# One scan stage of an encoder layer: smaller score blocks on TensorE, a mask moved within VectorE's order, and a subtraction moved to GpSimd

## What is computed

```
# one direction, per head: q, k, log f are 128 channels, v is 128 channels
b       = cumsum(log_f within the chunk)
o_inter = (q * exp(b)) @ state
scores  = q_t . k_s * exp(b_t - b_s)   for s <= t within the chunk, else 0
o       = o_inter + scores @ v
state   = exp(b_last) * state + (k * exp(b_last - b))^T @ v

kv      = rms_norm(memory) @ w_ckv     # 512 rows x 1024 times 1024 x 2048
```

## Time and profile before

| | us |
|---|---|
| median of 3 runs | 2024.71 (2020.85 to 2026.29) |
| the profiled execution | 2023.5 |
| its span, first to last instruction | 2021.7 |
| first and last TensorE work of `hgrn` | 460.25 to about 686.9 |

### The profile page before, as it was taken

One profiled execution on the slowest core, in us unless ns is written; L12 is line 12 of the kernel. 1 busy time (PEld: TensorE's weight loads), 2 busy tenths in 40 slices (PEclk: granted clock), 3 DMA queues, 4 the chain that ended last, 5 costly groups with the idle time before them and its releaser, 6 DMA issues. The chain is left out here.

```text
span 2021.7 us, 32126 instructions
## 1 busy us (share of the span) xinstructions
PE 1940.0 (96%) x11104; PEld 1609.6 (80%) x11104; DVE 1467.0 (73%) x2035; ACT 1225.7 (61%) x1962; POOL 277.2 (14%) x391
## 2 busy tenths in 40 slices
PE   7989999999999899999999999999999999999995
PEld 6878888887888676778888888887888888888882
DVE  5447765648999588877411355468999999999985
ACT  5453467427788488754222333336888888888873
POOL 0220012110000021111000000001222222222210
PEclk9999999999999999999999999999999999999997
DMA  6493334446565460343334523337999999999998
GB/s 207 162 313 109 105 115 146 151 172 180 181 183 178 151 199 27 116 135 134 115 120 138 163 84 110 116 132 272 384 386 382 384 378 382 380 386 383 394 370 323
DMA packets 177237, 441.98 MB, mean 219 GB/s; under 512 B 20768, under 2 KB 100000, under 8 KB 151264
## 3 DMA queue, kind: packets, MB, share of 16 engines
q1 hardware_dynamic: 145168, 341.19, 47.1%
q0 software_dynamic: 31952, 99.25, 13.3%
HBM read 359.64 MB, written 94.37 MB: 225 GB/s over the span
## 5 line engine op out<-in xcount | busy, mean ns | idle before, releaser
L113 PE MATMUL cross_ot_ps<-w_w_high,cross_o_high 128*128 128x512 f32 x528 | 213.4, 404 | 4.6 <-DVE w_w_low L2952 2.8
L115 PE MATMUL cross_ot_ps<-w_w_high,cross_o_low 128*128 128x512 f32 x528 | 207.1, 392 | 0.0
L2952 DVE TENSOR_TENSOR cross_low_up<-cross_raw_up,w_w_high 128x2048 fp32r<-128x2048 f32 x66 | 148.3, 2288 | 9.4 <-ACT w_w_high L2719 9.3
L2952 DVE TENSOR_TENSOR w_w_low<-cross_raw_gate,w_w_high 128x2048 fp32r<-128x2048 f32 x68 | 152.3, 2278 | 0.0
L2952 DVE TENSOR_TENSOR cross_low_down<-cross_raw_down,w_w_low 128x2048 fp32r<-128x2048 f32 x64 | 143.4, 2282 | 0.0
L2719 ACT ACTIVATE w_w_high<-cross_raw_gate 128x2048 fp32r<-128x2048 f32 x68 | 126.2, 1907 | 0.0
L113 PEld LDWEIGHTS cross_ot_ps<-w_w_high,cross_o_high 128*128 128x128 f32 x528 | 99.9, 189 | 29.9 <-DVE w_w_low L2952 7.1
L2719 ACT ACTIVATE w_w_high<-cross_raw_up 128x2048 fp32r<-128x2048 f32 x66 | 122.5, 1907 | 0.3 <-issue 0.3
L2719 ACT ACTIVATE w_w_low<-cross_raw_down 128x2048 fp32r<-128x2048 f32 x64 | 119.0, 1914 | 0.0
L115 PEld LDWEIGHTS cross_ot_ps<-w_w_high,cross_o_low 128*128 128x128 f32 x528 | 99.7, 189 | 21.5
L114 PE MATMUL cross_ot_ps<-w_w_low,cross_o_high 128*128 128x512 f32 x264 | 104.2, 395 | 0.0
(11 more groups left out here) (539 smaller groups left out, 5495.1 us busy)
## 6 DMA issues: line engine op xcount, KB each, us to landing
cross_raw_gate<-in_w_gate_dram SPq DMA_DIRECT2D x66, 1024.0 KB, 7.7
cross_raw_up<-in_w_up_dram SPq DMA_DIRECT2D x66, 1024.0 KB, 9.5
cross_raw_down<-in_w_down_dram SPq DMA_DIRECT2D x64, 1024.0 KB, 9.0
front_pair_raw<-in_w_in_dram SPq DMA_DIRECT2D x9, 1024.0 KB, 7.0
cross_y_kept<-y_rows SPq DMA_DIRECT2D x16, 512.0 KB, 10.4
front_raw<-in_w_in_dram SPq DMA_DIRECT2D x10, 512.0 KB, 5.5
k_t<-front_staged POOLq DMA_DIRECT2D x20, 256.0 KB, 2.7
lf_t<-front_staged_lf POOLq DMA_DIRECT2D x20, 256.0 KB, 3.0
```

What stands on the lines that cost most here:

```text
L113: pe.matmul(out, lhs[0], rhs[0], start=first, stop=False)
L115: return pe.matmul(out, lhs[1], rhs[0], start=False, stop=last)
L2952: dve.tensor_tensor(w_low[s][:, cols], raw[s][:, cols], w_high[s][:, cols].bitcast(F32), ALU.subtract).then_inc(w_low_done[s], 1)
```

## The change

Six edits, all in `hgrn`:

1. Level scores are computed only where they are not zero: one 64x64 block per head at level 64, two 32x32 blocks per head at level 32. Level 16 stays at four 32x32 blocks per head, each with its zeros. Each block has `start=True` and `stop=True`, and there is no adding up over levels.
2. The centred scores are four 32x32 blocks per head in place of one 128x128.
3. The level scores have a PSUM buffer for each direction and the centred scores a bank of their own. Both are set to zero once by VectorE at the start of the stage (two memsets, 128x1024 and 128x512), for the parts that no block writes. TensorE waits for them before slot 0.
4. GpSimd sets 4 halves to zero in place of 12.
5. `decayed` is cut in two, `decayed_levels` (the six half multiplies) and `decayed_rest`, and `mask(n+1)` is put between them, where before `mask(n+1)` came first in the next slot.
6. `split_low` is done by GpSimd for all of the parts 2 to 15, ahead of the DMA of part p - 2.

```diff
-        kt_ps, o_ps, st_ps = (m.ps(s, [P, HW]) for s in ("kt_ps", "o_ps", "st_ps"))
-        s_ps = m.ps("s_ps", [P, 2, 2, HEADS // 2, P])
+        kt_ps, o_ps, st_ps, centred_ps = (m.ps(s, [P, HW]) for s in ("kt_ps", "o_ps", "st_ps", "centred_ps"))
+        levels_ps = m.ps("levels_ps", [P, 2, HW])
 ...
             def _(pool):
                 for t, half in ((q_dec, early), (k_dec, late)):
                     for u in range(2):
-                        for j, w in enumerate(LEVELS):
-                            halves = t[:, u, j].rearrange("p (g two l) -> p g two l", two=2, l=w)
-                            pool.memset(halves[:, :, half[u]], 0.0).then_inc(zeros_done, 1)
+                        halves = t[:, u, n_lev - 1].rearrange("p (g two l) -> p g two l", two=2, l=base)
+                        pool.memset(halves[:, :, half[u]], 0.0).then_inc(zeros_done, 1)
+
+                def split_low(p):
+                    pool.wait_ge(w_high_done, p - 1)
+                    pool.tensor_tensor(w_low[p % 2][:], raw[p % 2][:], w_high[p % 2][:].bitcast(F32),
+                                       ALU.subtract).then_inc(w_low_done, 1)
+
                 for p in range(parts):
+                    if p + 2 < parts:
+                        split_low(p + 2)
 ...
-                    act.activation(by_head(s_t[:]), levels_ps, ACT.Copy).then_inc(level_scores_done, 1)
+                    act.activation(s_t[:], levels_ps[:, u], ACT.Copy).then_inc(level_scores_done, 1)
 ...
             def _(dve):
                 dve.sem_inc(base_done, PRIME)
+                dve.memset(levels_ps[:].rearrange("p u c -> p (u c)"), 0.0).then_inc(levels_zeroed, 1)
+                dve.memset(centred_ps[:], 0.0).then_inc(levels_zeroed, 1)
 ...
-                decayed(0, 0)
+                decayed_levels(0, 0)
+                decayed_rest(0, 0)
                 dve.memset(state[:], 0.0).then_inc(state_done, PRIME)
-                split_low(2)
                 differences(1, 0)
                 mask(0, 0)
-                decayed(0, 1)
-                split_low(3)
+                decayed_levels(0, 1)
+                decayed_rest(0, 1)
                 for n in range(slots):
-                    if n:
-                        mask(n // 2, n % 2)
                     if n + 3 < slots:
                         differences((n + 3) // 2, (n + 3) % 2)
                     carry(n // 2, n % 2)
                     if n + 2 < slots:
-                        decayed(n // 2 + 1, n % 2)
-                    for p in range(4, parts):
-                        if split_in[p] == n:
-                            split_low(p)
+                        decayed_levels(n // 2 + 1, n % 2)
+                    if n + 1 < slots:
+                        mask((n + 1) // 2, (n + 1) % 2)
+                    if n + 2 < slots:
+                        decayed_rest(n // 2 + 1, n % 2)
 ...
-                        pe.wait_ge(zeros_done, 4 * n_lev)
+                        pe.wait_ge(zeros_done, 4)
+                        pe.wait_ge(levels_zeroed, 2)
 ...
+                    def block(into, j, h, s_at, t_at, size):
+                        rows, cols = (slice(h * P + at, h * P + at + size) for at in (s_at, t_at))
+                        return pe.matmul(into[s_at:s_at + size, cols], k_dec[:, u, j, rows], q_dec[:, u, j, cols],
+                                         start=True, stop=True)
+
+                    wide, narrow = LEVELS[0], 2 * base
                     for h in range(HEADS):
-                        cols = slice(h * P, (h + 1) * P)
-                        pe.matmul(s_ps[:, h % 2, 1, h // 2], k_dec[:, u, n_lev, cols], q_dec[:, u, n_lev, cols],
-                                  start=True, stop=True)
-                    for pair in range(HEADS // 2):
-                        for j, w in enumerate(LEVELS):
-                            for h in (2 * pair, 2 * pair + 1):
-                                for at in range(0, P, 2 * w):
-                                    cols = slice(h * P + at, h * P + at + 2 * w)
-                                    done = pe.matmul(s_ps[at:at + 2 * w, h % 2, 0, pair, at:at + 2 * w],
-                                                     k_dec[:, u, j, cols], q_dec[:, u, j, cols],
-                                                     start=(j == 0), stop=(j == n_lev - 1))
+                        block(levels_ps[:, u], 0, h, early[u] * wide, late[u] * wide, wide)
+                    for h in range(HEADS):
+                        for at in range(0, P, 2 * narrow):
+                            block(levels_ps[:, u], 1, h, at + early[u] * narrow, at + late[u] * narrow, narrow)
+                    for h in range(HEADS):
+                        for at in range(0, P, narrow):
+                            block(levels_ps[:, u], n_lev - 1, h, at, at, narrow)
+                    for h in range(HEADS):
+                        for at in range(0, P, narrow):
+                            done = block(centred_ps, centred, h, at, at, narrow)
                     done.then_inc(scores_ready, 1)
```

More of the change, by code:

```diff
@@ L1167, in hgrn @@
         raw, w_high, w_low = zip(*early_split)
-        kt_ps, o_ps, st_ps = (m.ps(s, [P, HW]) for s in ("kt_ps", "o_ps", "st_ps"))
-        s_ps = m.ps("s_ps", [P, 2, 2, HEADS // 2, P])
-        by_head = lambda t: t.rearrange("p (a b t) -> p a b t", b=2, t=P)
-        levels_ps, centred_ps = (s_ps[:, :, c].rearrange("p b a t -> p a b t") for c in range(2))
+        kt_ps, o_ps, st_ps, centred_ps = (m.ps(s, [P, HW]) for s in ("kt_ps", "o_ps", "st_ps", "centred_ps"))
+        levels_ps = m.ps("levels_ps", [P, 2, HW])
         acc = m.ps("acc", [P, 2, 512])
@@ L1177, in hgrn @@
         o_stored = [m.sem(f"o_stored{u}") for u in range(2)]
-        (scan_done, zeros_done, diff_done, decay_done, base_done, scores_ready, level_scores_done, s_done,
-         kt_done, o_ready, o_done, state_done) = (
+        (scan_done, zeros_done, levels_zeroed, diff_done, decay_done, base_done, scores_ready,
+         level_scores_done, s_done, kt_done, o_ready, o_done, state_done) = (
             m.sem(s) for s in (
-                "scan_done", "zeros_done", "diff_done", "decay_done", "base_done", "scores_ready",
-                "level_scores_done", "s_done", "kt_done", "o_ready", "o_done", "state_done"))
+                "scan_done", "zeros_done", "levels_zeroed", "diff_done", "decay_done", "base_done",
+                "scores_ready", "level_scores_done", "s_done", "kt_done", "o_ready", "o_done", "state_done"))
         def token(i, u):
@@ L1356, in differences, with decayed_levels @@
                                       ALU.subtract).then_inc(diff_done, 1)
-                def decayed(i, u):
+                def decayed_levels(i, u):
                     n = 2 * i + u
@@ L1361, in decayed @@
                     if n == 0:
-                        dve.wait_ge(zeros_done, 4 * n_lev)
+                        dve.wait_ge(zeros_done, 4)
                     dve.drain()
@@ L1371, in decayed, with decayed_rest @@
                         dve.tensor_tensor(kd[:, :, early[u]], e[:, :, early[u]], halves(k)[:, :, early[u]], ALU.mult)
+                def decayed_rest(i, u):
+                    n = 2 * i + u
+                    q, k = x[i % 2][:, u, 0], x[i % 2][:, u, 1]
                     dve.tensor_tensor(q_dec[:, u, n_lev], q, decay[:, u, centred], ALU.mult)
@@ L1384, in mask @@
                     dve.wait_ge(level_scores_done, n + 1)
-                    dve.copy_predicated(by_head(s_t[:]), where_i[:, u].unsqueeze(1).unsqueeze(1).to_broadcast(
-                        [P, HEADS // 2, 2, P]), centred_ps).then_inc(s_done, 1)
+                    dve.copy_predicated(s_t[:].rearrange("p (h t) -> p h t", h=HEADS),
+                                        where_i[:, u].unsqueeze(1).to_broadcast([P, HEADS, P]),
+                                        centred_ps[:].rearrange("p (h t) -> p h t", h=HEADS)).then_inc(s_done, 1)
                 def carry(i, u):
```

## The result

The changed kernel takes 2028.5 us (2026.1 to 2033.2, 20 runs). The kernel before took 2022.8 us (2019.8 to 2028.7, 20 runs) beside it. The ratio is 1.0028 [1.0022, 1.0035], so the change costs 5.7 us. Forecast was +6.4 us. That is slower, but by a little less than the 0.3% that the prediction set as its bound: in its own classes the outcome is "within", to which it gave 0.35, and not "slower by more" (0.40).

What follows compares the result with a forecast made beforehand. Both engines were taken as nearly balanced, with VectorE the bound after the change. -22.2 us (splits off VectorE, waits, zeroing, shorter TensorE tail) plus 28.6 for GpSimd's subtractions gave +6.4, 2031.1 us; range 2001 to 2040, forecast's own 2027 to 2036.

Steps and rivals of the forecast that it cites:

- TensorE's slot: TensorE per slot of the stage: small blocks cut scores from 3.36 to 1.7 us, the slot by 1.65 to 9.04.
- Rival D: TensorE's scores: small blocks cost as much as large ones, slot stays 10.69 us, total 2034; chance 0.04.
- VectorE's slot without a split: VectorE from scan to scan in a slot with no split: 9.66 us, above TensorE's 9.04, so VectorE is the bound.
- Zeroing: Two PSUM memsets ahead of VectorE's first scan, all on the path: +1.5 us, between 0.9 and 2.
- What a subtraction costs VectorE: Each GpSimd split holds VectorE's two-input instructions for its whole 2.2 us; 13 splits give 28.6 us.
- A: Rival on GpSimd's splits: no exclusion over long instructions, no cost to VectorE, -22.2 us, 2002.5; chance 0.17.
- B: Rival on GpSimd's splits: VectorE held in part, 1.0 to 1.9 us each, mean 1.5, total 2022; chance 0.18.
- C: Rival: longer GpSimd subtraction or cold TensorE; 3.2 us each gives 2044, 2.7 gives 2038; chance 0.13.
- The sum: Whole stage: -22.2 us without any cost of GpSimd, +28.6 for its subtractions, together +6.4 us.
- The skill's rule: VectorE instructions with two SBUF inputs and GpSimd instructions reading SBUF exclude each other for a whole instruction.
- The mask's move, costed at nothing: VectorE's mask moves forward 2.48 us as the same work, without waiting for scores, 3.9 us in hand: cost nothing.
- TensorE needs the low part only after the eight units between, 13 us on.: GpSimd's split: TensorE uses its low part 13 us later, behind eight units of the product.

Runs made afterwards that it cites:

- e6: Changed kernel, but for parts 4 to 14 GpSimd starts its subtraction only after the slot's differences, beside `carry`; 2021.3 us, ratio 0.9997.
- e2: Changed kernel with GpSimd writing zeros of the same 128x1024 in place of the subtraction (not the whole work); 2005.2 us, ratio 0.9912.
- e3: Changed kernel with GpSimd copying the raw weights, one input read, in place of the subtraction (not the whole work); 2012.1 us, ratio 0.9947.
- e12: Changed kernel with splits on VectorE, those of parts 4 to 15 behind `carry`, and the mask back at the next slot's head; 2020.7 us, ratio 0.9985.
- e9: Changed kernel with splits back on VectorE, those of parts 4 to 15 directly behind `carry` instead of at the slot's end; 2017.0 us, ratio 0.9968.
- e1: Changed kernel with edit 6 alone undone: VectorE does the splits again at their old places; 2032.4 us, ratio 1.0048.

## Why the prediction held, and what it missed

- **TensorE's slot.** Predicted 9.04 us. The last two slots start their `output` at 680.66 and 689.64, 8.98 apart, with no wait between. The scores took 1.55 us against 1.7 predicted, 3.36 before:

```profile
499.47 1.33 PE L1454 MATMUL hgrn_levels_ps<-hgrn_q_dec,hgrn_k_dec 128*64 128x64 f32 x56
500.61 0.49 PE L1454 MATMUL hgrn_centred_ps<-hgrn_q_dec,hgrn_k_dec 128*32 128x32 f32 x32
501.02 0.50 PE L113 MATMUL hgrn_acc<-mem_high,mem_second_high 128*128 128x512 f32 x1
```

  Rival D is out.
- **VectorE's slot without a split.** Predicted 9.66; the scans at 598.76 and 608.40 are 9.64 apart.
- **Zeroing.** Predicted 1.5. The first scan starts 462.49 - 461.13 = 1.36 behind the first memset. Counted from GpSimd's first row of the stage it starts at 1.75 (460.74 to 462.49) where it was 0.15 before (459.90 to 460.05), so 1.6 later:

```profile
461.13 0.91 DVE L1337 MEMSET hgrn_levels_ps<- 128x1024 f32 x1 [2.14 <-PEq L91]
462.10 0.48 DVE L1338 MEMSET hgrn_centred_ps<- 128x512 f32 x1
462.49 1.16 DVE L1351 TENSOR_TENSOR_SCAN hgrn_b<-mem_head_start,mem_first_x 128x512 f32<-128x512 f32 x1
```

- **What a subtraction costs VectorE.** Predicted 2.2 us each, 28.6 in all. Six of the thirteen rows are about 2.20 above their like (as 500.76 above), and seven 1.95 (as 543.85 below). The sum is 6 x 2.20 + 7 x 1.95 = 26.9. Rivals A and B are out, and C's longer subtraction too. That the hold is 2.07 on average where 2.2 was forecast is in part luck. The forecast took the hold for GpSimd's whole duration, put at 2.2 us; the duration is 2.36 to 2.40 where nothing delays it (e6), and the hold is 0.2 to 0.4 us shorter than that. The two errors cancel. The forecast also had a second read set behind the first. The rows are 0.96 us for the write alone (e2), 1.04 to 1.07 with one input (e3) and 2.4 with two, so a second input does cost far more than the first, but why isn't shown.
- **The sum.** -22.2 + 26.9 = +4.7 with the measured term. The stage's last matmul ends at 692.09 + 0.39 = 692.5, 5.6 later than before, and 0.84 of that was there when the stage began (ScalarE and GpSimd start it at 460.74, before at 459.90). That leaves 4.8. The forecast "near 693" holds. The profiled span grew by 7.7 us; 2.1 of it lies behind the stage, where nothing was changed, and its cause is open.
- **The skill's rule.** The forecast took it from the Trainium skill (SBUF — State Buffer, section "Who interferes with whom") that the exclusion goes both ways. The 2.89 us row agrees, and so do e2 (a write doesn't contend) and `carry` in e6 (one input in SBUF doesn't).
- **The mask's move, costed at nothing.** It costs nothing (VectorE waits once, 1.6 us, for ScalarE's copy, in 20 masks), but it isn't worth nothing: e12 against e9 is 3.7 us. The step that failed looked only at what the mask waits for, not at who waits for the mask. In the forecast that sat inside the bound of VectorE and changed no term of the sum. The forecast named TensorE's wait for `base_done`; its wait for the mask is the larger one, 17.6 against 11.1.
- **"TensorE needs the low part only after the eight units between, 13 us on."** This failed, and the trace of the kernel before already spoke against it. There the split ends just as TensorE arrives:

```profile
534.00 1.22 DVE L1403 TENSOR_TENSOR mem_next_low<-mem_next_raw,mem_next_high 128x1024 fp32r<-128x1024 f32 x1
...
535.27 0.50 PE L113 MATMUL hgrn_acc<-mem_high,mem_next_high 128*128 128x512 f32 x1 [0.45 <-DVE mem_next_low L1403]
```

  In three of the 14 parts TensorE waited 0.44 to 0.45 us for it, and in a fourth the split ended 0.05 us ahead of it. With TensorE's slots shorter the same places become e1's waits: in three parts TensorE is there 5 us before a split that stands last in VectorE's slot. In the changed kernel GpSimd's low part is done at 535.02 and TensorE comes for it at 535.81, so it is in time by 0.8 us and not by 13. The failed step had no weight in the sum. But it hid a use of edit 6: the move also takes the split out of VectorE's order. That is why undoing it (e1) isn't faster, as a count of VectorE's time alone has it (13 x (2.07 - 1.13) = 12 us). Those 12 us are there only when the split also leaves the end of the slot (e9).

So the change is slower than before by 5.7 us because it pays 2.07 us of VectorE's time (26.9 / 13) to save 1.13 us of it, thirteen times, which is 12.2 us and more than the other edits bring. With the subtraction on VectorE behind `carry`, the same small blocks and order are 0.32% faster than before (e9). No run puts the split behind `carry` in the kernel before, so how much of this 0.32% is due to the blocks isn't shown.

## What to carry to other kernels

Here an elementwise operation with two inputs in SBUF, moved to GpSimd beside a VectorE that streams operations of two SBUF inputs, cost VectorE most of GpSimd's duration: 2.07 us (of 2.4) for the 1.13 it saved. Started beside work that reads PSUM it cost 1.2. Before such a move, compare the two numbers. And when an edit makes the consuming engine faster, go through everything that the other engine makes at the end of its order, small waits first: one of 0.45 us became one of 5.64 here, and behind it TensorE's granted clock was 0.54. Moving the producer 5.3 us forward in its engine's order left 0.3 of the wait.

## What was not expected of the hardware

How long GpSimd itself waits depends on when it arrives. At 500.51 it got in at VectorE's next instruction. Here it didn't:

```profile
541.33 0.69 DVE L1387 TENSOR_TENSOR hgrn_k_dec<-hgrn_x_odd,hgrn_to_end 128x512 f32<-128x512 f32 x1
541.93 0.69 DVE L1390 TENSOR_TENSOR hgrn_q_dec<-hgrn_x_odd,hgrn_from_start 128x512 f32<-128x512 f32 x1
542.54 1.22 DVE L1351 TENSOR_TENSOR_SCAN hgrn_b<-mem_head_start,mem_first_x 128x512 f32<-128x512 f32 x1
543.85 2.36 DVE L1358 TENSOR_TENSOR hgrn_diff<-hgrn_b 128x256 f32<-128x256 f32 x1
...
541.74 4.18 POOL L1246 TENSOR_TENSOR mem_second_low<-mem_second_raw,mem_second_high 128x1024 fp32r<-128x1024 f32 x1 [6.22 <-ACT mem_second_high L1301]
```

It arrives within L1387, and L1390 and the scan go ahead of it. It gets in only behind the scan, where VectorE has a gap of 0.09 us, and so its row is 4.18 us. VectorE is then held for 1.95. The prediction had GpSimd get in ahead of VectorE's next instruction each time; three rows of 4.17 to 4.18 and three of 3.51 to 3.69 are against that. It costs VectorE nothing more, so the sum held. All six that were passed over arrived while a 512-column product of `decayed_rest` ran (L1387 or L1390), and seven of the other eight while a half-width operation or a scan did. What lets it in at one border between instructions and not at another, no run here tells apart.
